# Two index-query weight tiles split on VectorE, the fourth tile rounded sooner, and the memory values in banks 4 and 5

## The reference, cut to what matters

```
x = first_block(...)                     # ends with rms_norm(h, norm_final_g)
h = rmsnorm(x, g_mix_pre)                # norm "n_mix2"
proj = h @ w_in                          # aq, ak, av, iq, ik, iw, bq, bk, bv, cq, gates
mkv = rmsnorm(mem, g_mem) @ w_mem_kv     # memory keys mk and memory values mv, 256 rows
s = einsum('bqhd,bkd->bqhk', iq, ik) * IDX_DIM ** -0.5
score = einsum('bqh,bqhk->bqk', iw, relu(s))     # the index scores, from which top_k chooses keys
```

## Time and profile before

| | us |
|---|---|
| median of 3 runs | 1771.84 |
| lowest and highest | 1770.43, 1775.9 |
| the profiled execution, its own time | 1774.14 |
| its span, first to last instruction | 1772.0 |
| TensorE busy in it | 1727.3 (97%) |
| GpSimd, VectorE, ScalarE busy | 676.1, 857.0, 629.0 |
| mean granted TensorE clock | 0.993 |

### The profile page before, as it was taken

One profiled execution on the slowest core, in us unless ns is written; L12 is line 12 of the kernel. 1 busy time (PEld: TensorE's weight loads), 2 busy tenths in 40 slices (PEclk: granted clock), 3 DMA queues, 4 the chain that ended last, 5 costly groups with the idle time before them and its releaser, 6 DMA issues.

```text
span 1772.0 us, 23230 instructions
## 1 busy us (share of the span) xinstructions
PE 1727.3 (97%) x7982; PEld 1361.9 (77%) x7982; DVE 857.0 (48%) x1373; ACT 629.0 (35%) x1011; POOL 676.1 (38%) x286
## 2 busy tenths in 40 slices
PE   7999999999999999999999999999999899999998
PEld 5788676788888888887688765668888588888887
DVE  6602665583655552217397766541323565555013
ACT  5233444433322223327424455443223422222122
POOL 2444222234544444435343000224444354444443
PEclk9999999999999999999999999999999899999999
DMA  4434311123333233324322111113332133332332
GB/s 170 157 121 127 105 50 60 49 95 96 119 95 95 95 97 105 95 95 130 123 84 84 48 37 36 60 36 99 102 95 95 48 114 100 95 95 95 95 98 69
DMA packets 47344, 162.25 MB, mean 92 GB/s; under 512 B 5692, under 2 KB 7868, under 8 KB 47016
## 3 DMA queue, kind: packets, MB, share of 16 engines
q1 hardware_dynamic: 43728, 151.16, 27.1%
q10 hardware_dynamic: 3544, 10.13, 1.7%
HBM read 156.91 MB, written 4.76 MB: 91 GB/s over the span
## 4 chain that ended last, share of the span: by engine, by line
PE 46%; issue 35%; POOL 13%; DVE 4%; ACT 1%; DMA 0%; POOLq 0%; SPq 0%; DVEq 0%; ACTq 0%
POOL w_lo L387 13%; PE ps L438 13%; PE ps L440 12%; PE ps L439 12%; PE ps L906 1%; PE ps L905 1%; PE ps L904 1%; PE ps L603 1%; PE ps L624 1%; PE ps L640 1%; PE ps L792 1%; DVE tmp L1961 1%; PE ps L834 0%; DMA w_raw<-stream 0%; DVE w_lo L1968 0%
## 5 line engine op out<-in xcount | busy, mean ns | idle before, releaser
L387 POOL TENSOR_TENSOR w_lo<-w_raw,w_hi 128x1024 fp32r<-128x1024 f32 x269 | 663.6, 2470 | 1070.3 <-ACT w_hi L975 1070.3
L438 PE MATMUL ps<-u_hi,w_hi 128*128 128x512 f32 x1376 | 558.0, 405 | 20.1 <-DVE u_lo L1574 5.7
L440 PE MATMUL ps<-u_hi,w_lo 128*128 128x512 f32 x1376 | 538.9, 392 | 0.0
L439 PE MATMUL ps<-u_lo,w_hi 128*128 128x512 f32 x1376 | 538.3, 391 | 0.0
L975 ACT ACTIVATE w_hi<-w_raw 128x1024 fp32r<-128x1024 f32 x278 | 292.6, 1055 | 414.8 <-PE ps L440 340.5
L438 PEld LDWEIGHTS ps<-u_hi,w_hi 128*128 128x128 f32 x1376 | 259.4, 189 | 98.2 <-issue 41.2
L440 PEld LDWEIGHTS ps<-u_hi,w_lo 128*128 128x128 f32 x1376 | 259.4, 189 | 55.7
L439 PEld LDWEIGHTS ps<-u_lo,w_hi 128*128 128x128 f32 x1376 | 259.8, 189 | 52.1 <-issue 2.6
L1865 DVE TENSOR_TENSOR a_lo<-tmp,a_hi 128x512 f32 (+1 forms) x44 | 116.4, 2646 | 4.7
L1316 ACT ACTIVATE tmp<-tmp 128x512 f32<-128x512 f32 x44 | 27.8, 632 | 222.6 <-DVEq L1855 222.6
L438 PE MATMUL ps<-a_hi,w_hi 128*128 (+1 forms) x264 | 102.9, 390 | 0.0
(11 more groups left out here) (332 smaller groups left out, 2276.6 us busy)
## 6 DMA issues: line engine op xcount, KB each, us to landing
w_raw<-stream SPq DMA_DIRECT2D x278, 512.0 KB, 3.4
g_rep<-g_one ACTq DMA_DIRECT2D x1, 2560.0 KB, 15.3
hT<-xT SPq DMA_DIRECT2D x4, 512.0 KB, 5.5
spread<-m_rows ACTq DMA_DIRECT2D x4, 512.0 KB, 4.6
tmp<-tmp ACTq DMA_DIRECT2D x32, 64.0 KB, 3.7
bias<-g_rep ACTq DMA_DIRECT2D x1, 2048.0 KB, 8.1
outT<-hT SPq DMA_DIRECT2D x16, 128.0 KB, 1.8
mem_in<-memT ACTq DMA_DIRECT2D x1, 1024.0 KB, 4.9
```

The source lines that it names most:

```text
L387: pool.tensor_tensor(w_lo[:, slot], w_raw[:, slot], w_hi[:, slot].bitcast(F32), ALU.subtract)\
L438: pe.matmul(out, wh, xh, start=start, stop=False)
L439: pe.matmul(out, wh, xl, start=False, stop=False)
L440: return pe.matmul(out, wl, xh, start=False, stop=stop)
```

## The change

Three things are changed. The low parts of units 135 and 136 (iq 0 and 1) are made by VectorE, one after the fourth `second_lo` tile and one after the eighth; GpSimd's ring leaves those two units out. ScalarE rounds unit 138 (iq 3) after the fifth tile of `u_hi`, where it did so after all eight. And the memory values go to banks 4 and 5; the scaled tiles of norm n_mix2 go to banks 6 and 7 instead, and the third and fourth iq results to 4 and 5.

```
@@ scaled
-            return [tmp[4], tmp[5], tmp[0], tmp[1]][k % 4][:, 0:MEM] if name == "n_mem" else ps[:, 4 + k % 2, :]
+            return [tmp[4], tmp[5], tmp[0], tmp[1]][k % 4][:, 0:MEM] if name == "n_mem" else \
+                ps[:, (6 if name == "n_mix2" else 4) + k % 2, :]
@@ GpSimd
             pool.wait_ge(lo_ready, 1)
-            ring(1, BY_VECTOR[0])
+            ring(1, FIRST["iq"])
+            pool.wait_ge(lo_ready, FIRST["iq"] + 2)
+            ring(FIRST["iq"] + 2, BY_VECTOR[0])
@@ TensorE
-                token_unit(FIRST["mv"] + j, j, [6, 7], um_hi, um_lo, (lambda: norm("n_mix2", T)) if j == 2 else None)
+                token_unit(FIRST["mv"] + j, j, [4, 5], um_hi, um_lo, (lambda: norm("n_mix2", T)) if j == 2 else None)
...
-            acquire(6)
+            acquire(4)
...
-                m = split_mm(ps[:, 6, :], w_hi[:, t % R, c], w_lo[:, t % R, c], u_hi[:, k], u_lo[:, k],
+                m = split_mm(ps[:, 4, :], w_hi[:, t % R, c], w_lo[:, t % R, c], u_hi[:, k], u_lo[:, k],
...
-            tile_unit(t + 1, (t + 1) % R, 7, u_hi, u_lo)
+            tile_unit(t + 1, (t + 1) % R, 5, u_hi, u_lo)
@@ ScalarE
-                        own.step(act.activation(mv[:, i], ps[:, 6 + i, :], ACT.Copy))
-                        act.sem_inc(bank_free[6 + i], 1)
+                        own.step(act.activation(mv[:, i], ps[:, 4 + i, :], ACT.Copy))
+                        act.sem_inc(bank_free[4 + i], 1)
                         act.sem_inc(named("mv_copied"), 1)
                 norm_hi_tile("n_mix2", u_hi, T, k)
+                if k == 4:
+                    feed_after(FIRST["iq"] + 1)
...
-            feed_after(FIRST["iq"] + 1)
             for j in (2, 3):
...
-                own.step(act.activation(iq[:, j, :], ps[:, 4 + j, :], ACT.Copy))
-                act.sem_inc(bank_free[4 + j], 1)
+                own.step(act.activation(iq[:, j, :], ps[:, 2 + j, :], ACT.Copy))
+                act.sem_inc(bank_free[2 + j], 1)
@@ VectorE
+            def index_weights(t):
+
+                dve.wait_ge(lo_ready, t)
+                dve.wait_ge(hi_ready, t + 1)
+                dve.tensor_tensor(w_lo[:, t % R], w_raw[:, t % R], w_hi[:, t % R].bitcast(F32), ALU.subtract)\
+                   .then_inc(lo_ready, 1)
+
             for k in range(KT):
+                if k == 4:
+                    index_weights(FIRST["iq"])
                 dve.wait_ge(named("second_hi"), k + 1)
...
+            index_weights(FIRST["iq"] + 1)
             norm_split("n_mix2", "mix2", lambda k: hT[:, k], T, u_hi, u_lo, KT // 2)
```

## The result

| | before | after |
|---|---|---|
| median, us | 1773.23 (8 runs) | 1767.25 (8 runs) |
| lowest and highest | 1770.43, 1775.9 | 1763.33, 1768.52 |
| ratio, 95% interval | | 0.9962, 0.995 to 0.9974 |
| the profiled execution: time, span | 1774.14, 1772.0 | 1765.62, 1763.8 |

The kernel became 0.38% faster by the ratio; the medians are 6.0 us apart (0.34%). The same kernel was run twice more among the experiments (16 executions), and before 66 times beside them; over all of them the means are 1773.6 and 1767.1 us, 6.5 apart.

The account below looks back on a forecast made before the run. TensorE, busy 97%, could win only its gaps and slow clock. From the median 1771.84, less 4.3 us of waits and 1.7 of clock, gives 1765.8, stated as 1766.0; range 1763.8 to 1769.4.

Parts of the forecast that it names:

- The first gap: TensorE idles 1.70 us before 809.47, standing at bank 7 for a key copy; 1.86 us lost, 1.70 more by the clock.
- Part 1: Memory values into banks 4 and 5: the bank 7 wait goes whole, gain 1.86 us, and 1.70 if the clock fell.
- Part 2: Low parts of iq 0 and 1 on VectorE, 1.2 us each; the scaled chain starts 1.9 us sooner from this.
- unhappy case: A VectorE low-part tile meeting GpSimd would cost up to 1.2 + 2.4 us and this part's gain would vanish.
- Part 3: Unit 138 rounded between fifth and sixth `u_hi`, costing 0 to 0.1 us; iq 3 starts at 835.4, 5.9 us sooner.
- The sum: Waits 4.6 us less 0.3 that stays, 4.3, plus clock 1.70: together 6.0 us from the profiled execution.
- the clock term: Two TensorE gaps removed, each costing a clock fall of 1.70 us about every second time: 1.7 us on average.
- rival (a): No clock gain in the medians, or falls turn up elsewhere equally; only the waits go, 4.3 us: 1767.5 us, 28%.
- (b): VectorE's chain isn't sooner than Part 1 alone puts it; iq 2 waits 1.9 us more: 1768.7 us, 15%.
- (d): The change doesn't do what it says in VectorE's and ScalarE's order; no time moved, 1771.8 us, 2%.
- Rival (c): Shifted later TensorE waits bring more clock falls, 1.70 us each; slower, 1777.7 us with six more, 4%.

Follow-up runs that it names:

- sooner: Against before, only the rounding of unit 138 is moved ahead of the sixth `u_hi`; ratio 0.9984, passage 48.8 us.
- banks: Against before, only the banks of mv, the third and fourth iq results and the scaled tiles are moved; ratio 1.0005, passage 51.8 us.
- held: Against before: banks and sooner rounding, both low parts on GpSimd, the second waiting for VectorE's eighth `second_lo` tile; ratio 0.9961, passage 46.8 us.
- vector: Against before, only the low parts of iq 0 and 1 go to VectorE; ratio 0.998, passage 50.2 us.
- vector_sooner: The changed kernel with the bank edit taken back; ratio to before 0.9974, passage 48.0 us.
- all_three: The changed kernel itself, run again beside the single parts; ratio to before 0.997, passage 46.2 us.
- all_again: The changed kernel itself a second time, in a third session; ratio to before 0.9961, passage 46.2 us, median 1767.07.
- banks_vector: The changed kernel with the sooner rounding of unit 138 taken back; ratio to before 0.9968, passage 48.2 us.
- busy: The changed kernel plus constant matmuls, three before and six after the norm matmul behind `out2`; ratio to before 0.9963, passage 46.2 us.

## Why the prediction was right, step by step

**The first gap (Part 1).** Gone as forecast, the clock at 1.00 behind it. One piece was missed: the first mv matmul itself had waited about 0.3 for bank 6, which the key copy before the last one frees. In the earlier trace rows only bank 7 has a bracket; the 0.3 shows as 806.44 to 806.85, against 805.58 to 805.70 now. And the 2.0 us by which Part 1 was to bring the chain forward hold only beside a fall: between executions without one it is 0.6 (sooner 18.5 us after the last key matmul, banks 17.9). The prediction did not separate the two. Unit 134 and the norm matmul came where said: shifting the forecast by the 0.86 that after is ahead, 813.0 against 812.93, with 0.24 of waiting instead of 0.1.

**The low parts (Part 2).** Forecast 1.22 us each; 1.21 measured. Forecast start of the scaled chain 821.7 on the shifted clock; 821.41 measured. iq 0 at 818.0; 817.97 measured. What held the tiles was read rightly off the three ends 0.55 after GpSimd's, and held bears it out, since it gets most of the gain without moving the work. The Trainium skill ("SBUF — State Buffer", "Who interferes with whom") states this exclusion, and here every held tile agrees. Its unhappy case, a weight tile of VectorE that meets GpSimd, was not seen: GpSimd rested for 10.5 us.

**The sooner rounding (Part 3).** Forecast at 828.8, measured 828.48; low part ready at 832.3, measured 832.0. iq 3 starts at 834.35; forecast 834.5.

**The sum.** 6.0 in all was forecast. In the passage it was 6.2 by the two profiles, 4.5 of it waits (4.3 forecast; the 0.3 at bank 6 is most of the difference) and 1.7 the fall in before's profile. The medians also moved by 6.0. That this agrees to a tenth is in part luck: it needs the clock term, which is the weakest one, and the time named, 1766.0, was 1.3 below the 1767.25 measured, since the median of before that it was counted from was 1.4 low. Taken as a time and not as a difference, 1767.25 lies nearer to the 1767.5 of rival (a). Rivals (b) and (d) are out by the traces. Rival (c), more falls, didn't come.

**The clock term is the soft one.** It was 1.7 on average, from two gaps with even odds, and the odds were taken from three waits. The trace of before has two longer ones, 2.48 us before 55.98 and 2.79 before 189.71, with no fall behind them, which the prediction left out. All 13 profiles together have 19 waits of 1.47 to 1.73 us: four at bank 7, three before iq 3, twelve in the attention between 1010 and 1020 us. The clock fell behind six of them (two, one and three). With odds of about one in three the term is 2 x 0.32 x 1.7 = 1.1 us instead of 1.7.

The mean clocks point to the same size and leave it open. Over all executions the mean clock is 0.9927 in before (66) and 0.9934 in the changed kernel (24), 0.0007 apart, give or take 0.0005. A fall of 3.4 us is 0.001 and costs 1.7 where TensorE is at work, so this would be 1.2 us, 0.3 to 2.0, if all of it lay on the path; the falls near 56 us and around 1390, which the change has no part in, are in these means too. Rival (a) in its strict form, no clock gain, is unlikely but not out.

Which gap costs the clock is not known. By the mean clocks it is not the wait for bank 7: the kernels which still have it (vector, sooner, vector_sooner) do not have a lower clock (0.9934 to 0.9938) than those without. Only before and banks are low (0.9927, 0.9922), and these two have both waits at iq 2 and iq 3, 0.4 and 1.7 us within 4 us. But in the profiles the clock fell behind the wait for bank 7 in two of four (before, vector), and behind that of iq 3 in one of three (banks). No run was made to settle it.

**The total.** Of the 6.5 us between the means, 4.5 are waits of the passage and about 1.2 the clock; some 0.8 stay without a place. The sessions alone differ by more than that: the means lie 5.7 apart in the session of all_three and 7.0 in that of all_again.

## What to carry to other kernels

When a gap is set by its own chain, list the chains before you remove the gap: here three cures gave 0.6, 2.1 and 1.9 us alone and each cost 1.8 to 2.0 when left out, and the banks, whose wait of 1.7 us was as long as any in the list, gave no time alone. A VectorE instruction with a duration far above its twins, ending just behind a GpSimd instruction, is a hint that the two should be kept apart, by moving the work or by a wait. And ask whether slow-clock time is on the path before you work on it.

## What the runs showed of the hardware

- A VectorE instruction that reads two SBUF operands and starts beside a GpSimd `tensor_tensor` ends about 0.55 us after it: 1.88 to 2.94 us instead of 0.74 (before, after). One with a PSUM operand ran beside GpSimd at 0.68 to 0.76 (before, after).
- Of 19 waits of 1.47 to 1.73 us at TensorE in 13 profiles, six were followed by a fall to 1.2 GHz (before at 809.7 and 1017.9, vector at 809.2, banks at 842.3, banks_vector at 1015.1, all_again at 1011.3). In the same program places others were not (sooner at 810.5, after at 1010.4).
- Filling the 8 us of idleness around a norm kept TensorE at 2.4 GHz there (mean clock 0.9960 in busy against 0.9932 in all_three) with no gain in time that could be seen.
